# Norm products of a delta-rule head: one full-precision product or two single-pass ones, and their place in the level inverse

## The reference, cut to what matters

```python
def l2_normalize(t):
    return t * lax.rsqrt(jnp.sum(t * t, axis=-1, keepdims=True) + 1e-6)

def gated_deltanet_mixer(q, k, v, beta, log_decay):
    q = l2_normalize(q.astype(f32)) * HEAD_DIM ** -0.5
    k = l2_normalize(k.astype(f32))
    ...
    sol = lax.linalg.triangular_solve(eye + lower, rhs, left_side=True, lower=True, unit_diagonal=True)
    ...
```

## Time and profile before

| | |
|---|---|
| median of 3 runs | 2877.76 us (2877.55 to 2878.59) |
| profiled execution | 2880.95 us |
| its span | 2879.4 us |
| mean granted TensorE clock | 0.998 of full |
| busy, share of the span | TensorE 99%, VectorE 57%, ScalarE 36%, GpSimd 14% |

### The profile page before, as it was taken

How to read it: one execution, slowest core, us unless ns; L and a number is a source line. 1 busy time by engine, 2 the same in 40 slices (tenths; PEclk the granted TensorE clock), 3 DMA queues, 4 the chain that set the end, 5 groups by cost and what they waited for, 6 DMA issues and landing times.

```text
span 2879.4 us, 38309 instructions
## 1 busy us (share of the span) xinstructions
PE 2840.2 (99%) x14864; PEld 2371.0 (82%) x14864; DVE 1640.5 (57%) x1683; ACT 1050.8 (36%) x1143; POOL 405.8 (14%) x438
## 2 busy tenths in 40 slices
PE   8999999999999999999999999999999999999997
PEld 5888777788889988898888888888888888888886
DVE  7445777655454442534534433343343798888888
ACT  5323433423453332432424323223233333333334
POOL 4000000000001133200011233233223200000001
PEclk9999999999999999999999999999999999999999
DMA  5333232233347764423423555556556756555555
GB/s 166 95 81 90 74 82 63 63 90 83 110 138 229 225 200 124 175 86 105 146 73 88 164 178 191 178 170 197 179 166 202 270 219 219 205 217 215 207 210 133
DMA packets 453647, 439.80 MB, mean 153 GB/s; under 512 B 9104, under 2 KB 365488, under 8 KB 453424
## 3 DMA queue, kind: packets, MB, share of 16 engines
q1 hardware_dynamic: 424288, 344.56, 39.0%
q0 software_dynamic: 29264, 93.90, 9.2%
HBM read 360.31 MB, written 75.50 MB: 151 GB/s over the span
## 4 chain that ended last, share of the span: by engine, by line
PE 91%; DVE 3%; DMA 2%; ACT 2%; issue 1%; POOL 0%; SPq 0%; DVEq 0%; ACTq 0%
PE slab_ps L855 19%; PE slab_ps L856 18%; PE slab_ps L857 18%; PE down_ps L1439 6%; PE down_ps L1440 6%; PE down_ps L1441 6%; PE down_ps L855 2%; PE mix_ps L856 2%; PE mix_ps L857 2%; PE mix_ps L855 2%; PE down_ps L857 2%; PE down_ps L856 2%; PE mix_ps L909 1%; PE mix_ps L916 1%; DMA w_raw<-in_w_cross_kv_dram 1%
## 5 line engine op out<-in xcount | busy, mean ns | idle before, releaser
L855 PE MATMUL slab_ps<-act_hi,w_hi 128*128 128x512 f32 (+2 forms) x2704 | 1023.6, 379 | 16.7 <-DVE act_lo L2117 10.9
L857 PE MATMUL slab_ps<-act_hi,w_lo 128*128 128x512 f32 (+2 forms) x2704 | 1000.9, 370 | 0.0
L856 PE MATMUL slab_ps<-act_lo,w_hi 128*128 128x512 f32 (+2 forms) x2704 | 1000.7, 370 | 0.0
L2065 DVE TENSOR_TENSOR w_lo<-w_raw,w_hi 128x2048 fp32r<-128x2048 f32 x200 | 469.2, 2346 | 370.6 <-ACT w_hi L1465 369.9
L855 PEld LDWEIGHTS slab_ps<-act_hi,w_hi 128*128 128x128 f32 (+1 forms) x2704 | 509.9, 189 | 110.8 <-issue 25.0
L857 PEld LDWEIGHTS slab_ps<-act_hi,w_lo 128*128 128x128 f32 (+1 forms) x2704 | 509.6, 188 | 87.8 <-issue 0.6
L856 PEld LDWEIGHTS slab_ps<-act_lo,w_hi 128*128 128x128 f32 (+1 forms) x2704 | 510.2, 189 | 84.6 <-issue 5.1
L1465 ACT ACTIVATE w_hi<-w_raw 128x2048 fp32r<-128x2048 f32 x200 | 382.0, 1910 | 513.3 <-PE slab_ps L857 394.4
L1439 PE MATMUL down_ps<-half_hi,u_slot 128*128 128x512 f32 x896 | 349.8, 390 | 1.9 <-DVE half_lo L2795 1.9
L1441 PE MATMUL down_ps<-half_lo,u_slot 128*128 128x512 f32 x896 | 349.7, 390 | 0.0
L1440 PE MATMUL down_ps<-half_hi,u_slot 128*128 128x512 f32 x896 | 349.6, 390 | 0.0
(11 more groups left out here) (402 smaller groups left out, 3053.5 us busy)
## 6 DMA issues: line engine op xcount, KB each, us to landing
w_raw<-in_w_mlp_up_dram SPq DMA_DIRECT2D x64, 1024.0 KB, 6.7
b<-in_w_mlp_down_dram SPq DMA_DIRECT2D x64, 1024.0 KB, 7.0
w_raw<-in_w_in_dram SPq DMA_DIRECT2D x56, 1024.0 KB, 5.6
u_slot<-u_park SPq DMA_DIRECT2D x112, 512.0 KB, 8.3
w_raw<-in_w_cross_kv_dram SPq DMA_DIRECT2D x32, 1024.0 KB, 6.3
u_park<-u_hi POOLq DMA_DIRECT2D x32, 896.0 KB, 9.0
u_park<-u_lo POOLq DMA_DIRECT2D x32, 896.0 KB, 8.9
w_raw<-in_w_mix_out_dram SPq DMA_DIRECT2D x16, 1024.0 KB, 5.9
```

Source lines behind the costliest of these rows:

```text
L855: mm(ps, wh, xh, start=first, stop=False)
L856: mm(ps, wh, xl, start=False, stop=False)
L857: return mm(ps, wl, xh, start=False, stop=last)
L2065: tt(w_lo[:, slot], w_raw[:, slot], f32(w_hi[:, slot]), ALU.subtract).then_inc(on["slab_lo"], 1)
```

## The change

The sum over the partitions becomes two single-pass fp32r products, one of the squares rounded and one of their rests. ScalarE makes each square twice, once in fp32 and once rounded (`dn_sq_hi`, which lies where `sq` and `nrm` lie); VectorE subtracts (`delta_square_rests`, in place of the fp32 squares) behind `take_v(5)` and ahead of the convolution of v, and ahead of the loop behind the silus. TensorE's norm products move from level 5 to level 6 of the inverse, with one hop more behind level 5. ScalarE's inverse roots move from ahead of the `dn_uw` evictions to behind them. A new semaphore `dn_sqhi` orders the subtraction, and `dn_sq` is now counted by VectorE. Two unused semaphore names go.

```diff
--- before.py
+++ after.py
@@ -107,7 +107,7 @@
 o_sq xg_hi act_ready act_free o_add mem_sq mem_add mem_total mem_rstd x_parked
 mem_back y_back mem_hi mem_split bcast_ps dist_ready gate_clamped gate_sig gate_ready o_ready sq_ready sq_hi
 norm_sum norm_ready vt_ready vtok_ready ret_rot ret_qk ret_scores ret_w dn_clamped dn_sig dn_silu dn_sq dn_l2
-dn_inv dn_qk dn_dd dn_dt dn_masked dn_at dn_pair dn_tok dn_x dn_zero dn_ct dn_u dn_uev dn_v dn_uw dn_uwev dn_eg
+dn_inv dn_qk dn_dd dn_dt dn_masked dn_tok dn_sqhi dn_x dn_zero dn_ct dn_u dn_uev dn_v dn_uw dn_uwev dn_eg
 dn_qg dn_ws dn_vnew dn_ds dn_state gla_z gla_l gla_qs gla_diag gla_d gla_e gla_qe gla_lv gla_lvout gla_topout
 bcast_rows dn_gram dn_bvk dn_gbev dn_cols sb_scores sb_x sb_masked sb_l sb_lk sb_cum sb_z sb_w
 xsq_ready xacc_ready cx_scores cx_max cx_exp cx_p cx_pt pt_hi pt_ready vo_hi out_mul out_added up_in u_squared u_summed
@@ -274,6 +274,8 @@
             osq = sb("osq", [P, 4, S])
             sb("mixers_below", [P, 20 * S])
             oacc = sb("oacc", [P, S])
+        with ExitStack() as scope:
+            dn_sq_hi = [alloc(scope)(f"dn_sq_hi{n}", [P, S], F32R)[:] for n in range(2)]
         sb = alloc(mix)
         sq = sb("sq", [P, S])
         nrm = sb("nrm", [P, S])
@@ -293,6 +295,12 @@
             ret_t = sb("ret_t", [P, 2, S])
             ret_sq = sb("ret_sq", [P, 2, S], F32R)
             ret_wt = sb("ret_wt", [P, PK])
+        with ExitStack() as scope:
+            sb = alloc(scope)
+            dn_sq_lo = []
+            for n, below in enumerate((1, 6)):
+                sb(f"dn_below{n}", [P, below, S])
+                dn_sq_lo.append(sb(f"dn_sq_lo{n}", [P, S], F32R)[:])
         with ExitStack() as scope:
             sb = alloc(scope)
             dn_rows = sb("dn_rows", [P, S], F32R)
@@ -961,9 +969,10 @@
 
             def delta_norms(hd):
 
-                for n, t in enumerate((dn_gb, dn_dt)):
+                for n in range(2):
                     pe.wait_ge(on["dn_sq"], hd * 2 + (n + 1))
-                    mm(M[n][:], ones[:], t[:], start=True, stop=True).then_inc(on["dn_l2"], 1)
+                    mm(M[n][:], ones_round[:], dn_sq_hi[n], start=True, stop=False)
+                    mm(M[n][:], ones_round[:], dn_sq_lo[n], start=False, stop=True).then_inc(on["dn_l2"], 1)
 
             def delta_first():
 
@@ -1041,11 +1050,11 @@
                                   halves_of(tile(dn_xt, c), n, 1), start=True, stop=True)
                     last.then_inc(on["dn_v"], 1)
                     if n == 5:
+                        for _ in range(3):
+                            yield HOP
+                    else:
                         yield HOP
                         delta_norms(hd + 1)
-                        yield HOP
-                    else:
-                        yield HOP
                         yield HOP
 
                 pe.wait_ge(on["dn_x"], hd * 7 + 7)
@@ -1587,7 +1596,8 @@
             def delta_squares(hd):
                 for n, t in enumerate((dn_gb, dn_dt)):
                     act.wait_ge(on["dn_silu"], hd * 3 + (n + 1))
-                    fn(t[:], dn_c[:, n], ACT.Square).then_inc(on["dn_sq"], 1)
+                    fn(t[:], dn_c[:, n], ACT.Square)
+                    fn(dn_sq_hi[n], dn_c[:, n], ACT.Square).then_inc(on["dn_sqhi"], 1)
 
             def delta_norms(hd):
                 for n, t in enumerate((dn_gb, dn_dt)):
@@ -1635,11 +1645,11 @@
                 take_u(5)
                 delta_squares(hd + 1)
                 take_u(6)
-                delta_norms(hd + 1)
                 act.wait_ge(on["dn_uw"], hd + 1)
                 chain.put(fn(dn_uu[:], M[2][:], ACT.Copy))
                 chain.sync()
                 fn(dn_wt[:], M[3][:], ACT.Copy).then_inc(on["dn_uwev"], 1)
+                delta_norms(hd + 1)
                 yield SEG
                 delta_silu(hd + 1, 2, dn_temp[2])
                 gate_sigmoid(heads.at())
@@ -2213,6 +2223,11 @@
                     dve.wait_ge(on["dn_sig"], hd * 3 + (t + 1))
                     tt(dn_c[:, t], dn_c[:, t], dn_temp[t][:], ALU.mult).then_inc(on["dn_silu"], 1)
 
+            def delta_square_rests(hd):
+                for n in range(2):
+                    dve.wait_ge(on["dn_sqhi"], hd * 2 + (n + 1))
+                    tt(dn_sq_lo[n], (dn_gb, dn_dt)[n][:], f32(dn_sq_hi[n]), ALU.subtract).then_inc(on["dn_sq"], 1)
+
             def delta_scaled(hd):
 
                 dve.wait_ge(on["dn_silu"], hd * 3 + 3)
@@ -2238,6 +2253,7 @@
                 for t in range(2):
                     delta_conv(0, 0, t)
                 delta_silu(0, (0, 1))
+                delta_square_rests(0)
                 chain.link(v.memset(dn_rows[:].bitcast(F32), 0.0))
                 delta_rows(0)
                 yield SEG
@@ -2342,6 +2358,7 @@
                 delta_silu(hd + 1, (0, 1))
                 yield HOP
                 take_v(5)
+                delta_square_rests(hd + 1)
                 delta_conv(1 - par, hd + 1, 2)
                 take_v(6)
                 tt(flat3(dn_at[:]), flat3(dn_at[:]), every_tile(tri_incl[:]), ALU.mult).then_inc(on["dn_masked"], 1)
```

## The result

| | before | after |
|---|---|---|
| median of 12 runs | 2878.51 us | 2885.07 us |
| range | 2877.55 to 2881.12 | 2883.79 to 2886.35 |
| ratio | | 1.0023, 95% interval 1.0016 to 1.0030 |
| span of the profiled execution | 2879.4 us | 2883.4 us |

The change makes the kernel 6.6 us slower; +6.05 was forecast. The norm products are shorter in the loop, and TensorE idles in places where it did not before. The page of the changed kernel: TensorE is busy for 98% of the span instead of 99%, and ScalarE and VectorE hold 7% of the chain that ended last instead of 5%.

The account below looks back on a forecast made before the run. TensorE, busy 99% of the span, was taken to bound the kernel. First execution +2.05 us plus four heads at +1.0 each gave +6.05 on 2877.76, so 2883.8 us; own range 2882.8 to 2884.7, wider range 2880.8 to 2885.3.

Parts of the forecast that it names:

- TensorE's saving: Norm products: four single-pass products take 0.93 us instead of 1.72, saving 0.79 per execution, 3.95 over five.
- The estimate of 1.2: Norm products at the skill page's 131 ns: four cost 0.52 us, saving 1.2 per execution; the forecast kept the trace's 0.233.
- Level six and the rests in the loop: Inverse, levels five to six: one hop changes sides, nothing spills; VectorE's two subtractions of 0.69 us are hidden by 1.5.
- The roots' place: ScalarE behind `dn_uw` evictions: split 1.4 us late, state copy late, TensorE waits; +1.0 per head after the saving, +4.0 total.
- the 0.1 at L1080: TensorE's request for the inverse roots, then L1071: a wait up to 0.1 us, swallowed by the longer one three hops later.
- The first execution: Norms ahead of the loop: nothing hides the rests, VectorE's delay reaches TensorE whole, +2.05 us, bounds +0.3 to +2.2.
- Sum: Whole kernel: 2.05 + 4 x 1.0 = +6.05 us, giving 2883.8 us, +0.21%.
- (a): Rival: ScalarE's late split costs nothing, only the first execution does; -1.1 us, 2876.7; chance 0.09.
- (b): Rival: all new work on the other engines is hidden; -3.95 us, 2873.8; chance 0.05.
- (c): Rival: the recurrence waits but the first execution does not; +3.2 us, 2881.0; chance 0.12.
- (d): Rival: TensorE's clock falls in the new waits, one dip a head; +6 us more, 2889.9; chance 0.07.
- (e): Rival: the clock dip at 558 or the loop's turn falls otherwise; -1.5 or +1.3 us, 2882.3 or 2885.1; chance 0.12.

Follow-up runs that it names:

- e2: Changed kernel with inverse roots back ahead of the `dn_uw` evictions and the execution ahead of the loop in old form; medians -3.24 us against the kernel before.
- e1: Changed kernel with the inverse roots back ahead of the `dn_uw` evictions; medians -0.73 us, stage -1.23 us against the kernel before.
- e4: Kernel before with one edit, the inverse roots moved behind the `dn_uw` evictions; medians +4.40 us, stage +4.26 us against the kernel before.
- e6: Changed kernel with VectorE's copy of the first state moved ahead of `w_lo`; medians +1.47 us, stage +1.37 us against the kernel before.
- e7: e1 with head 0's two rests subtracted by GpSimd and its products five hops later; medians +0.94 us against the kernel before.
- e8: e7 with GpSimd's rests held until VectorE has written head 0's rows, head 0's products three hops later; medians -2.26 us against the kernel before.
- e5: e2 with the four single-pass products of each head moved back to level five; medians +1.00 us, stage +1.21 us against the kernel before.

## Why the prediction was right, point by point

**TensorE's saving, 0.79 each.** Held for the four in the loop. Four products took 0.92 (0.93 forecast), and e2 gives 3.17 for four executions, 0.79 each; inside a head it is 28.17 - 27.39 = 0.78. The estimate of 1.2 from the 131 ns of the Trainium skill (TensorE: Matmul & The Clock Gate, Back-to-back issue gap) would have made it 4.8.

**Level six and the rests in the loop cost nothing.** Held (e1, e2). In the changed kernel VectorE's level-six eviction starts at 339.16 without idle, for VectorE is busy up to it, and ends at 339.57; TensorE's `dn_uw` products at 341.07 did not wait for it.

**The roots' place.** Held. The split 1.4 late was worked out; it starts 346.67 - 342.83 = 3.84 later, of which 2.07 is head 0 and 0.38 the trace's start, which leaves 1.39. For the first state product the forecast was a wait of 1.7 and 0.1 for the weight load; shown are 1.48 of idle. The idle counts from the modelled end of the product before, 0.39 behind its start, while the slot is 0.23, so 1.48 is 1.64 of lost time, and the product is 0.49 long instead of 0.39. Sum 1.74 against 1.8; the heads themselves show 29.17 - 27.39 = 1.78, which less the 0.78 saved is +1.00. e4 shows it alone, e6 shows the path through VectorE's queue. Nothing of the 0.1 at L1080, where the roots were asked for at the last moment, can be seen.

**The first execution.** Held at 2.07, forecast 2.05. Of the parts, TensorE idles 0.38 and 0.30 at the products and 1.11 at the transposes, which are 1.68 later than before (about 1.9 forecast). The rest arrives at a slab product at 307.57, which idles 0.20 up to `blk_x`, a wait that the forecast did not name: the product behind it is 2.07 later (308.47 against 306.02), and so is L1038, whose idle of 0.33 is as long as before.

**Sum.** By the stage, 5.92 - 2.07 = 3.85 for four heads, 0.96 each where 1.0 was forecast. Inside the heads it is 1.00; the stage also holds the idle at the loop's turn, which was 0.81 after and 1.33 before, and waits for `dn_xt` of 1.4 in all against 1.2. The medians show 6.56; the 0.64 between them and the stage is within the interval, and no row accounts for it. The level of 2883.8 was 1.3 too low: 0.75 of that is the kernel before, whose 12 runs have a median of 2878.51 where its three had 2877.76.

**The rivals.** (a) and (b) needed the split in time for the state copy, and it was 1.4 late. (c) fell with the wait at L900. (d) did not happen: over all four waits of 1.5 the granted clock stayed 1.00 (2.4 GHz), as the row behind the loop's turn had suggested. But the mechanism is real: behind e7's wait of 2.85 it fell to 0.50, and that cost 1.3. What decides between the two is not shown. The Trainium skill (TensorE: Matmul & The Clock Gate, HAM oscillation — how this bites in real kernels) tells of a kernel whose waits for data are longer than the work between them and whose clock falls at every one; no run here has that pattern, since a head has 29.17 us of work to a wait of 1.48. (e) happened in the profile of before: the dip at 558 to 561 is missing in the ten other profiled executions, and it made the difference of spans 1.57 too small. A stretch of the changed kernel's execution around one of the waits (columns: stretch, length and TensorE's busy time with its instructions, granted clock, DMA share, GB/s):

```profile
349.00:351.20 2.20, 0.72 (x4) 1.00 0.00 0
```

## What to carry to other kernels

An engine's hole is only worth its place in the queue: moving 2.6 us of roots from a hole of 5 us on ScalarE to behind the next eviction put it ahead of the weight split, two queues away from the engine that paid. Before a step is moved in a hand-ordered queue, follow what stands behind it in each queue up to TensorE; work saved on TensorE ahead of a fixed arrival only becomes waiting. And where new work stands ahead of a loop with nothing to hide it, leave the first execution in its old form. Last, count a wait by more than its idle time, and look at the granted clock behind it: 2.85 us of waiting in e7 cost another 1.3.

## What the runs showed of the hardware that was not expected

- VectorE's instruction with a per-row scalar nearly stands still while GpSimd subtracts or clears: 0.48 became 1.41 and 2.81 (e7) and 1.48 (e8). A subtraction of two tiles on VectorE went from 2.29 to 2.77, and GpSimd's own from 1.29 to 3.31.
- A wait of TensorE costs more than the idle that the profile shows for it. 0.16 is the modelled end of the product before (0.39 behind its start, in a slot of 0.23), and 0.1 the weight load that is no longer hidden. By the length of a head, 0.39 is missing in e5 (1.09 for 0.70), 0.30 in e6 (0.65 for 0.35), 0.30 in the changed kernel (1.78 for 1.48) and 0.29 in e4 (1.13 for 0.84); 0.13 of the first and 0.03 to 0.04 of the others are not accounted for.
- The granted clock fell to 1.2 GHz behind a wait of TensorE of 2.85 us (e7) and stayed at 2.4 GHz behind waits of 1.48 (the changed kernel). In the profiled execution of the kernel before it also fell at 558 us, while TensorE was busy, in a stretch where the same work kept 2.4 GHz in the ten others.
